# The order in which an MoE kernel takes its experts, now computed in the routing step

## The reference

```python
logits = (t @ w_router + b_router).astype(jnp.float32)
top_vals, top_idx = lax.top_k(logits, TOP_K)          # 4 of 32
gate = jax.nn.softmax(top_vals, axis=-1)
...
h = xb @ w_up[e] + b_up[e]                            # 1024 -> 2048
g = jnp.minimum(h[:, :D_FF], SWIGLU_LIMIT)
lin = jnp.clip(h[:, D_FF:], -SWIGLU_LIMIT, SWIGLU_LIMIT)
act = g * jax.nn.sigmoid(SWIGLU_ALPHA * g) * (lin + 1.0)
return act @ w_down[e] + b_down[e]                    # 1024 -> 1024
```

## Time and profile before

| what | us |
|---|---|
| median of 3 runs | 2228.92 |
| lowest and highest run | 2226.05, 2230.78 |
| the profiled execution, its own time | 2227.35 |
| its span, first to last instruction | 2225.6 |
| PE busy in the span | 2126.1 |
| DVE busy | 1610.5 |
| ACT busy | 1211.4 |
| mean DMA rate | 243 GB/s |

### The profile page before, as it was taken

One profiled execution on the slowest core, in us unless ns is written; L12 is line 12 of the kernel. 1 busy time (PEld: TensorE's weight loads), 2 busy tenths in 40 slices (PEclk: granted clock), 3 DMA queues, 4 the chain that ended last, 5 costly groups with the idle time before them and its releaser, 6 DMA issues.

```text
span 2225.6 us, 33282 instructions
## 1 busy us (share of the span) xinstructions
PE 2126.1 (96%) x10402; PEld 1765.4 (79%) x10403; DVE 1610.5 (72%) x1858; ACT 1211.4 (54%) x1251; POOL 587.9 (26%) x589
## 2 busy tenths in 40 slices
PE   7999987997899999999999999999999999999996
PEld 6887987686588888888888878887888888878785
DVE  4688977447855665778698675977976887677766
ACT  4423262331545554666577564757755676565655
POOL 1001031106511111334053050513511252131404
PEclk9999999997899999999999999999999999999998
DMA  7123275512976765979699795988986898777967
GB/s 186 58 86 139 86 164 190 185 57 86 351 260 215 226 223 179 338 246 373 228 359 378 233 331 180 362 284 286 364 310 224 284 369 308 244 244 282 309 238 271
DMA packets 287303, 541.66 MB, mean 243 GB/s; under 512 B 37302, under 2 KB 53798, under 8 KB 286146
## 3 DMA queue, kind: packets, MB, share of 16 engines
q1 hardware_dynamic: 262866, 495.07, 63.9%
q0 software_dynamic: 24368, 45.72, 8.2%
HBM read 513.61 MB, written 65.13 MB: 260 GB/s over the span
## 4 chain that ended last, share of the span: by engine, by line
PE 55%; issue 6%; DVE 6%; ACT 3%; DMA 3%; ACTq 0%; DVEq 0%; POOL 0%; SPq 0%; POOLq 0%
PE ex_ps_l L2945 7%; PE ex_ps_l L2944 7%; PE ex_ps_g L2944 6%; PE ex_ps_g L2945 6%; PE ex_ps_y L2944 5%; PE ex_ps_y L2945 5%; PE ex_ps_l L2948 4%; PE ex_ps_g L2948 4%; PE ex_ps_y L2948 3%; DVE ex_w_lo L2711 3%; PE ex_ps_t L2882 2%; ACT ex_w_hi L2579 2%; DMA ex_late<-in_w_down_dram 2%; PE ex_ps_t L2892 2%; PE ex_ps_g L2954 1%
## 5 line engine op out<-in xcount | busy, mean ns | idle before, releaser
L2711 DVE TENSOR_TENSOR ex_w_lo<-ex_late,ex_w_hi 128x2048 fp32r<-128x2048 f32 x204 | 464.2, 2291 | 222.5 <-ACT ex_w_hi L2579 154.7
L2411 POOL TENSOR_TENSOR ex_passed<-keep_ident 128x1 f32<-128x1 f32 x136 | 125.7, 924 | 1102.2 <-ACT ex_y L2622 1077.9
L2579 ACT CAST ex_w_hi<-ex_late 128x2048 fp32r<-128x2048 f32 x170 | 324.5, 1909 | 115.7 <-PE ex_ps_g L2945 60.7
L2711 DVE TENSOR_TENSOR ex_w_lo<-keep_sig_o,ex_w_hi 128x2048 fp32r<-128x2048 f32 x136 | 309.6, 2288 | 100.1 <-ACT ex_w_hi L2579 100.1
L2579 ACT CAST ex_w_hi<-keep_sig_o 128x2048 fp32r<-128x2048 f32 x134 | 255.1, 1904 | 120.6 <-PE ex_ps_l L2945 37.0
L2944 PE MATMUL ex_ps_l<-ex_w_hi,ex_x_hi 128*128 128x512 f32 x784 | 308.6, 394 | 2.0 <-DVE ex_w_lo L2711 2.0
L2944 PE MATMUL ex_ps_g<-ex_w_hi,ex_x_hi 128*128 128x512 f32 x784 | 306.5, 391 | 3.8 <-DVE ex_w_lo L2711 2.1
L2945 PE MATMUL ex_ps_l<-ex_w_lo,ex_x_hi 128*128 128x512 f32 x784 | 305.5, 390 | 0.0
L2945 PE MATMUL ex_ps_g<-ex_w_lo,ex_x_hi 128*128 128x512 f32 x784 | 305.1, 389 | 0.0
L2944 PE MATMUL ex_ps_y<-ex_w_hi,ex_h_hi 128*128 128x512 f32 x544 | 217.3, 400 | 1.2 <-DVE ex_h_lo L2747 0.9
L2945 PE MATMUL ex_ps_y<-ex_w_lo,ex_h_hi 128*128 128x512 f32 x544 | 212.1, 390 | 0.0
(11 more groups left out here) (507 smaller groups left out, 4114.2 us busy)
## 6 DMA issues: line engine op xcount, KB each, us to landing
keep_sig_o<-in_w_up_dram SPq DMA_DIRECT2D x102, 1024.0 KB
ex_late<-in_w_up_dram SPq DMA_DIRECT2D x102, 1024.0 KB
ex_late<-in_w_down_dram SPq DMA_DIRECT2D x102, 1024.0 KB
keep_weights<-in_w_up_dram SPq DMA_DIRECT2D x68, 1024.0 KB
keep_sig_o<-in_w_down_dram SPq DMA_DIRECT2D x34, 1024.0 KB
st_tab<-tabs SPq DMA_DIRECT2D x8, 1408.0 KB, 12.4
keep_weights<-in_w_in_dram SPq DMA_DIRECT2D x5, 1024.0 KB, 5.5
pr_late_pieces<-in_w_in_dram SPq DMA_DIRECT2D x5, 1024.0 KB
```

The costliest lines, as they stand in the source:

```text
L2411: pool.tensor_tensor(passed[:, :], ident[:, 0:1], ident[:, 0:1], ALU.add).then_inc(passed_done, 1)
L2579: nc.scalar.copy(w_hi[:, j % SPLIT, :, :], raw(j)).then_inc(hi_done, 1)
L2711: v.tensor_tensor(w_lo[:, j % SPLIT, :, :], raw(j), w_hi[:, j % SPLIT, :, :].bitcast(F32), ALU.subtract).then_inc(lo_done, 1)
```

## The change

The routing now computes a turn for each expert, and a word for each turn. Experts 0 and 31 keep their places. Of the thirty in between, those with one block (of at most 128 tokens) and those with more alternate, each kind in order of its number, the latter first; if one kind runs out, the other follows alone. The word holds the body's bits as before, the expert (bits 3 to 7), whether it has three blocks (bit 8), its pass number (bits 9 on), and from bit 15 the same of the next turn, so that the next expert stands at bit 18. The engines take expert and next expert from the word, by shifts and masks. With the numbers above the order is

The work of each pass, its chunks and its blocks are as before. The diff, cut to its core:

```diff
+                def take_turns():
+                    pe.wait_ge(work_spread, 1)
+                    pe.matmul(psV, spread_work, ident[0:E, 0:E], start=True, stop=True).then_inc(in_turn_ready, 1)
...
-                for j in range(4, 7):
+                for j in range(4, 6):
                     bias(j)
+                take_turns()
+                bias(6)
                 turn_gates(2)
...
                 def plan_with_bias():
-                    step(v.tensor_copy(cnt_f[:, :], psC[0:1, :]))
+                    step(v.tensor_copy(cnt_f[:, :], psC[0:E, :]))
...
+                    step(v.tensor_tensor_scan(pairs[:, mid], zero[0:E, mid], two[:, mid], 0.0, ALU.add, ALU.add))
...
+                    step(v.scalar_tensor_tensor(work_a, three, 258.0, work_0[:, :], ALU.mult, ALU.add))
+                    step(v.tensor_copy(turn_at, iota_e[0:E, :]))
                     add_bias(3)
                     steps_done()
...
-                    step(v.scalar_tensor_tensor(plan_b[:, :], three[:, :], -6.0, plan_a[:, :], ALU.mult, ALU.add))
+                    step(v.tensor_tensor(ahead_of[:, mid], iota_e[0:E, mid], pairs_ahead[:, mid], ALU.subtract))
+                    step(v.scalar_tensor_tensor(pair_turn[:, mid], pairs_ahead[:, mid], alone, pairs_ahead[:, mid], ALU.min, ALU.add))
                     step(v.tensor_scalar(ord_2[:, :], ord_x[:, :], 2.0, float(E), ALU.mult, ALU.add))
+                    step(v.scalar_tensor_tensor(work, over, -3.0, work_b, ALU.mult, ALU.add))
+                    steps_done()
+                    step(v.scalar_tensor_tensor(alone_turn[:, mid], ahead_of[:, mid], all_pairs, ahead_of[:, mid], ALU.min, ALU.add))
...
+                    steps_done()
+                    link(v.scalar_tensor_tensor(turns_by[:, mid], pair_turn[:, mid], 1.0, alone_turn[:, mid], ALU.add, ALU.subtract))
+                    link(v.tensor_tensor(turns_by[:, mid], turns_by[:, mid], two[:, mid], ALU.mult))
+                    link(v.tensor_tensor(turn_at[:, mid], alone_turn[:, mid], turns_by[:, mid], ALU.add))
+                    link(v.scalar_tensor_tensor(selected, turn_at, turn_no[:, 0:1], work, ALU.is_equal, ALU.mult))
+                    link(v.tensor_reduce(in_turn_col, selected, AX.X, ALU.add))
+                    v.tensor_copy(spread_work, in_turn_col.to_broadcast([E, E])).then_inc(work_spread, 1)
                     add_bias(5)
+                    v.wait_ge(in_turn_ready, 1)
...
                     add_bias(6)
                     steps_done()
+                    step(v.tensor_tensor_scan(threes_turn, zero[0:1, 0:E], three_turn, 0.0, ALU.add, ALU.add))
+                    step(v.scalar_tensor_tensor(word_next[:, 0:E - 1], in_turn[:, 1:E], 32768.0, pass_0[:, 0:E - 1], ALU.mult, ALU.add))
+                    step(v.tensor_copy(word_next[:, E - 1:E], pass_0[:, E - 1:E]))
+                    steps_done()
+                    link(v.scalar_tensor_tensor(word_a, threes_turn, 512.0, in_turn, ALU.mult, ALU.add))
+                    link(v.scalar_tensor_tensor(word_b, three_turn, -512.0, word_a, ALU.mult, ALU.add))
+                    link(v.tensor_tensor(keep["plan"][:, :], word_b, word_next, ALU.add))
                     add_bias(7)
...
-        def passes(eng, e, body):
-
-            plan = eng.value_load(keep["plan"][0:1, bass.ds(e, 1)], min_val=1, max_val=8 * 2 * E + 7)
-            n = eng.snap(plan >> 3)
+        def passes(eng, turn, body):
+
+            plan = eng.value_load(keep["plan"][0:1, bass.ds(turn, 1)], min_val=1, max_val=2 ** 24 - 1)
+            n = pass_no(eng, plan)
+            e = eng.snap((plan >> 3) & (E - 1))
...
-                            skip = follows | three_blocks(pool.value_load(
-                                keep["plan"][0:1, bass.ds(e + 1, 1)], min_val=1, max_val=8 * 2 * E + 7))
+                            skip = follows | three_blocks_next(plan)
...
-                with act.Fori(0, E - 1) as e:
-                    passes(act, e, one_pass)
+                with act.Fori(0, E - 1) as turn:
+                    passes(act, turn, one_pass)
```

More of the change, by code:

```diff
@@ L1614, in project_out_route @@
         square = split_q[:, D:D + HALF]
-        two, three, threes, plan_a, plan_b, plan_c, over, over_1 = (
-            split_q[0:1, 2 * D - (i + 1) * E:2 * D - i * E] for i in range(8))
-        overs = split_q[0:1, 2 * D - 11 * E:2 * D - 8 * E].rearrange("p (w e) -> p w e", w=3)
+        (two, three, threes, work_a, work_b, work, over, over_1, pairs, pairs_ahead, alone_turn, pair_turn, ahead_of,
+         turns_by, turn_at) = (split_q[0:E, i * E:(i + 1) * E] for i in range(15))
+        overs = split_q[0:E, 15 * E:18 * E].rearrange("p (w e) -> p w e", w=3)
+        selected, spread_work = split_q[0:E, 18 * E:19 * E], split_q[0:E, 19 * E:20 * E]
+        in_turn, three_turn, threes_turn, word_a, word_b, word_next = (split_q[0:1, i * E:(i + 1) * E] for i in range(20, 26))
+        alone, in_turn_col = split_q[0:E, 26 * E:26 * E + 1], split_q[0:E, 26 * E + 1:26 * E + 2]
         weighted = split_q[:, D + HALF:D + HALF + K4 * E].rearrange("p (k e) -> p k e", k=K4)
@@ L1658, in project_out_route @@
         t_t = t_dram.rearrange("(j p) d -> p j d", p=P)
[L1659 removed]
+        CONSTS = 12 + WAVES - 1 + 8
         PLACES_AT = 3
@@ L2055, in plan_with_bias @@
                     add_bias(3)
                     steps_done()
-                    step(v.scalar_tensor_tensor(plan_a[:, :], threes[:, :], 8.0, plan_0[:, :], ALU.mult, ALU.add))
+                    all_pairs = pairs[:, E - 2:E - 1]
+                    step(v.tensor_tensor(pairs_ahead[:, mid], pairs[:, mid], two[:, mid], ALU.subtract))
+                    step(v.tensor_scalar(alone, all_pairs, -1.0, float(E - 2), ALU.mult, ALU.add))
                     step(v.tensor_tensor(ord_x[:, :], ord_f[:, :], acts, ALU.subtract))
-                    step(v.tensor_tensor(over[:, :], over_1[:, :], overs[:, 2, :], ALU.add))
+                    step(v.tensor_tensor(over, over_1, overs[:, 2, :], ALU.add))
@@ L2298, in three_blocks, with following @@
         def three_blocks(plan):
-            return (plan >> 1) & paired(plan)
+            return (plan >> 8) & 1
         def single_follows(e, plan):
             return 1 if e is LAST_E else (plan & 2) >> 1
+        def following(eng, e, blocks, plan):
+            if e is LAST_E:
+                return e
+            after = eng.snap(next_expert(plan))
+            if blocks == 1:
+                return after
+            return nc.s_assert_within(eng.snap(after + single_follows(e, plan) * (e - after)), 0, E - 1,
+                                      skip_runtime_bounds_check_because="one of two experts")
         def last_passes(eng, body):
             e = LAST_E
-            plan = eng.value_load(keep["plan"][0:1, e:e + 1], min_val=1, max_val=8 * 2 * E + 7)
-            n = eng.snap(plan >> 3)
+            plan = eng.value_load(keep["plan"][0:1, e:e + 1], min_val=1, max_val=2 ** 24 - 1)
+            n = pass_no(eng, plan)
             with eng.If((plan & 1) > 0):
@@ L2389, in _ @@
                     sp.dma_start(bias_rows[i * E:(i + 1) * E, :], p["b_up"][0]).then_inc(bias_in, 16)
-                with sp.Fori(0, E - 1) as e:
-                    passes(sp, e, one_pass)
+                with sp.Fori(0, E - 1) as turn:
+                    passes(sp, turn, one_pass)
                 sp.wait_ge(h3_out, 16 * TT)
@@ L2504, in one_pass @@
                     second = pool.snap(own + three_blocks(plan) + 1)
-                    after = pool.snap(e * COLS + COLS - follows * (COLS - 1))
+                    if e is LAST_E:
+                        after = pool.snap(own + 1) if kind is AHEAD else None
+                    elif blocks == 1:
+                        after = pool.snap(next_expert(plan) * COLS)
+                    else:
+                        beyond = pool.snap(next_expert(plan) * COLS)
+                        after = nc.s_assert_within(pool.snap(beyond + follows * (own + 1 - beyond)), 0, E * COLS - 2,
+                                                   skip_runtime_bounds_check_because="one of two columns of the table")
                     if kind is AHEAD:
@@ L2843, in one_pass @@
                 def one_pass(n, e, blocks, plan, kind=AHEAD, small=False):
-                    e_next = e + 1 - single_follows(e, plan) if blocks == 2 else e + 1
-                    item(v.snap(n), kind, blocks, e, e_next, small)
-                with v.Fori(0, E - 1) as e:
-                    passes(v, e, one_pass)
+                    item(v.snap(n), kind, blocks, e, following(v, e, blocks, plan), small)
+                with v.Fori(0, E - 1) as turn:
+                    passes(v, turn, one_pass)
                 last_passes(v, one_pass)
```

85 lines of the change are left out of this document (51 added, 34 removed).

## The result

The changed kernel takes 2245.67 us (median of 5 runs, 2240.82 to 2250.31), the kernel before 2228.92 (5 runs, 2226.05 to 2230.78): a ratio of 1.0078, 95% interval 1.0059 to 1.0098. It is slower, as forecast, but by 16.8 us in place of 10, and lies just above the range. The profiled span is 2243.0 us, 17.4 more than before.

The account below looks back on a forecast made before the run. TensorE was taken as busy for 2126.1 of 2225.6 us, with 12.2 us of loop waits bounding any reordering gain; 6.8 + 1.5 + 2.9 = 11.2 us on 2227.35 gave 2238.6, forecast 2239, range 2231 to 2245.

Parts of the forecast that it names:

- Junctions: Singles behind another expert's small pair: chunk 3 is cast late; five more such passes at 1.37 us, 6.8 us.
- Routing: End of the routing on VectorE: small instructions grow from 19 to 39, all exposed, 2.9 us.
- Register work: Two more ScalarE register operations at the head of ten singles behind small pairs, 0.15 us each pass, 1.5 us.
- Leaving the loop: TensorE's 2.09 us stop at expert 31's first matmul: no change, bounds -2.1 and +2.1 us.
- fetched again at each change of body: Rival: changes between pair and single bodies, 30 against 20, each fetch code; 21 us more, 2260 us; chance 0.03.
- New waits with no cause at starts of passes: Sign on TensorE's timeline that would show the prediction wrong; no size given.
- alternation helps: Rival: full buffers behind pairs end TensorE's waits for hidden rows and low parts, 10.4 us; 2219.9 us; chance 0.04.
- its lag is absorbed: Rival: VectorE and ScalarE catch up without TensorE noticing, only the routing's 2.9 us stays; 2230.3 us; chance 0.13.
- In a pair VectorE is mostly idle: Argument given for the rival of the absorbed lag, about VectorE in pair passes; no size given.

Follow-up runs that it names:

- run 4: Changed kernel with ScalarE's cast of the next pass's chunk 3 moved ahead of the last output rows: 2231.58 us, ratio 1.0014 to the kernel before.
- run 2: Changed kernel with turns from a table set by POOL, holding the old order 0 to 31: 2238.36 us, ratio 1.0046 to the kernel before.
- run 3: Changed kernel with a table of turns: expert 0, fifteen singles, fifteen with pairs, then 31: 2229.94 us, ratio 1.0004 to the kernel before.
- run 5: Changed kernel with the alternating order from a table, turns 2 and 3, and 29 and 30, exchanged: 2245.70 us, ratio 1.0072 to the kernel before.
- run 10: Changed kernel with idle semaphore increments at program starts, 97 on VectorE and 118 on ScalarE, shifting their code: 2239.38 us, ratio 1.0070 to the kernel before.
- run 9: Kernel before with idle semaphore increments at program starts, 31 on VectorE and 10 on ScalarE, shifting their code: 2227.68 us, ratio 1.0021 to it unshifted.
- run 11: Changed kernel's code with singles first, then pairs, and ScalarE's cast of chunk 3 moved ahead: 2220.95 us, ratio 0.9996 to the kernel before.
- run 1: Changed kernel with the same alternating order taken from a table set by POOL, computation kept: 2248.04 us, ratio 1.0086 to the kernel before.
- run 6: Kernel before with ScalarE's cast of the next pass's chunk 3 moved ahead of the last output rows: 2220.93 us, ratio 0.9968 to it unmoved.
- run 8: Changed kernel with ScalarE's cast and VectorE's low part of the next pass's chunk 3 both moved ahead: 2232.27 us, ratio 1.0014 to the kernel before.
- run 12: Changed kernel with ScalarE's cast moved, neighbours swapped at both ends and VectorE's code shifted by 97: 2222.64 us, ratio 1.0006 to the kernel before.

## Why the prediction was right in direction and short by 7 us

- **Junctions, 6.8 us: right.** Five were added, ten stand there, 38.13 to 38.22 each, and run 4 took all ten away by the very cause that was named. 6.5 measured.
- **Routing, 2.9: right,** 3.05. The Trainium skill's rule that semaphores between chained instructions cost nothing ("VectorE: DVE Perf Modes", section "The DRAIN you can't avoid") would have given 1.8; the rows at 0.21 decide against it again.
- **Register work, 1.5: wrong.** ScalarE's idle time at the head did grow, from 1.52 to 1.61, and the wait for the low part from 0.40 to 0.47 each, but the wait for the hidden rows later in the pass shrank from 0.49 to 0.46 (8.4 and 7.8 over 17). In run 2 the five junctions sum to 6.8, 0.3 less than before. The two more operations of ScalarE are not found in the length of the passes.
- **Leaving the loop, 0 with bounds of 2.1: the term that was mis-sized.** It costs 1.6 in the stall and 1.9 in the last pass, 3.5. The step that failed is "a single stands before it in place of a small pair: no change": TensorE's stop hangs on what stands before it (runs 2, 3 and 5), and a stop of 3.7 us has half the clock behind it, which no term had. Of the last pass's 1.9, either the half clock or ScalarE's stop for code would be enough (runs 2, 4 and 10).
- **The first pass and turn 2, not in the sum: 5.6.** The prediction looked for code only as something that is fetched again at each change of body, 21 us, and gave it 0.03. It was right to doubt that: from 697 to 2165 us no packet of code is fetched in either kernel, and the changes cost nothing. (It counted 20 changes in the old loop; 19 are there, and one is at its exit.) What it missed is that the first turns and the exit have a price that depends on where VectorE's and ScalarE's code lies (runs 9 and 10), and for TensorE on the order (run 5). The trace of before had the sign: a stop of 1.8 us with no cause behind the first pair and one of 2.09 at the exit. The chance of their growing with new code was left at zero.
- "New waits with no cause at starts of passes" was named as what would prove the forecast wrong, and they are what was found.
- The rivals in which alternation helps, or its lag is absorbed, are refuted by run 3 and by the ten passes. "In a pair VectorE is mostly idle", which spoke for the absorbed lag, was misread: in expert 14's it is busy for 37.1 of 68 us, in expert 12's for 38.6 of 58.
- The numbers agree in part by luck: the 1.5 that isn't there makes up for some of the 9.1 that the sum didn't have.

## What to carry to other kernels

Before changing an order for the sake of a queue, look for the pair of neighbours that costs more than the sum of its parts, and ask which engine's instruction stands behind a slow one only by position. Moving that one (a cast ahead of an output copy) was worth 7 us in the old order and 14 in the new. After it two orders of the same code lay 4 us apart (runs 4 and 11), in place of 18 (runs 1 and 3).

In a program with large bodies behind branches, price the first turns and the exit: search the profile for stops with no releaser there, and look in the same window for packets of the queues that bring instructions. Here the waits in stretches without such packets all had another cause. These stops came and went by microseconds when instructions were added far ahead of them, so a change of some tenths of a per cent should be compared with the old code merely shifted.

## What the runs showed of the hardware

- **Code has a place.** Forty-one instructions without any effect, more than 500 us ahead of the loop, made the kernel 0.21% slower (0.11 to 0.30), by a stop of 5.15 us on VectorE and one of 3.75 on ScalarE. TensorE's own stops, behind the first pair and at the exit, were 1.6 to 3.8 us. The Trainium skill ("Advanced Engine Details and Errata", section "ISA Cache") gives the sizes of the code cache, with lines of 16 KB. The trace agrees for one of the two queues, q8, which moved 0.61 MB of code in 37 packets; q14 moved 0.26 MB in 32, 8 KB each.
- **A loop of large bodies ran without fetching code.** Both kernels change between bodies, the new one 30 times, and neither has a packet of code from 697 to 2165 us.
- **TensorE's clock after a stop.** Behind idle times of 2.73, 3.73 and 3.96 us the granted clock was 0.50 to 0.58 of full for 3.6 to 5.4 us. At some 2 us it goes either way: 1.00 behind 1.95 us in run 2, and 0.60 behind 1.93 us in run 6. So the same stop can cost 1.6 us more or not, and a stop that grew from 2.1 to 3.0 over its pass cost 2.6 in all.
- **Behind a removed stop stood another limit.** In run 8 the work put ahead of VectorE's stop left it where it was, and the next chunk was late. In runs 10 and 12, with the code shifted, the stop was gone, and TensorE waited 2.6 and 3.4 us in the same pass for work that a late transfer held up.
